# Zero products until the first weights, four banks for the transform, another order of low parts, and the last expert's output by halves

## The reference

```
h = x
layer 0:  h += fourier_mixer(rms_norm(h))        # h @ w_in, 2-D FFT over tokens and 256 channels of a group, real part, @ w_out
          h += (silu(n @ w_gate) * (n @ w_up)) @ w_down          # n = rms_norm(h), 2816 hidden
layer 1:  h += neighbourhood_attention(rms_norm(h))              # 16 heads, 4 x 64 grid, window 16 wide, bias table, @ w_o
          logits = n @ w_router + b_router; top 2 of 8 experts, gates = softmax of the two
          h += sum over the two of gate * (silu(n @ Wg[e]) * (n @ Wu[e])) @ Wd[e]     # 3584 hidden
return rms_norm(h) * final_norm
```

## Time and profile before

| | us |
|---|---|
| three runs | 1366.85, 1367.61, 1368.39 |
| median | 1367.61 |
| the profiled execution | 1367.15 |
| its span | 1365.3 |

### The profile page before, as it was taken

The page is one execution under the profiler, slowest core; times in us unless marked ns, Lnnn a source line. Parts: engine busy times, 40 slices in busy tenths (PEclk is TensorE's granted clock), DMA queues, the critical chain, the costliest instruction groups (busy, mean ns, idle before and its releaser), DMA issues.

```text
span 1365.3 us, 17406 instructions
## 1 busy us (share of the span) xinstructions
PE 1344.7 (98%) x6341; PEld 1117.9 (82%) x6341; DVE 1111.9 (81%) x815; ACT 923.2 (68%) x755; POOL 34.5 (3%) x48
## 2 busy tenths in 40 slices
PE   8999999999999999999999999999999999999997
PEld 7888888787878888888888888888888888888885
DVE  5756666655678889888988988898898889889997
ACT  6554444545647778777777877877787787777774
POOL 0000000000101000000000000000000000002000
PEclk8999999999989999999999999999999999999999
DMA  9666775563339999999999999999999999999992
GB/s 354 246 207 179 210 211 190 175 204 104 101 109 378 383 378 365 395 382 357 398 388 372 373 394 377 358 398 388 368 376 394 367 370 397 381 374 385 396 394 90
DMA packets 194971, 432.32 MB, mean 317 GB/s; under 512 B 19632, under 2 KB 22064, under 8 KB 194800
## 3 DMA queue, kind: packets, MB, share of 16 engines
q1 hardware_dynamic: 178784, 416.28, 83.4%
q0 software_dynamic: 3360, 11.78, 2.2%
q10 hardware_dynamic: 12784, 3.69, 1.8%
HBM read 425.94 MB, written 5.78 MB: 316 GB/s over the span
## 4 chain that ended last, share of the span: by engine, by line
PE 95%; DVE 3%; ACT 1%; issue 1%; DMA 0%; POOL 0%; DVEq 0%; ACTq 0%
PE bank_G L1250 10%; PE bank_G L1252 10%; PE bank_G L1251 10%; PE bank_U L1250 10%; PE bank_U L1252 10%; PE bank_U L1251 10%; PE bank_Y L1250 8%; PE bank_Y L1252 8%; PE bank_Y L1251 8%; PE bank_T L1696 2%; PE bank_T L1250 1%; PE bank_T L1252 1%; PE bank_T L1251 1%; DVE w_lo L753 1%; PE bank_G L1512 0%
## 5 line engine op out<-in xcount | busy, mean ns | idle before, releaser
L753 DVE TENSOR_TENSOR w_lo<-raw,w_hi 128x2048 fp32r<-128x2048 f32 x390 | 885.9, 2289 | 184.6 <-ACT w_hi L458 183.8
L458 ACT ACTIVATE w_hi<-raw 128x2048 fp32r<-128x2048 f32 x390 | 748.6, 1920 | 276.6 <-PE bank_U L1252 98.2
L1250 PE MATMUL bank_Y<-w_hi,hidT_hi 128*128 128x512 f32 x492 | 192.2, 391 | 0.0
L1252 PE MATMUL bank_Y<-w_hi,hidT_lo 128*128 128x512 f32 x492 | 191.6, 389 | 0.0
L1251 PE MATMUL bank_Y<-w_lo,hidT_hi 128*128 128x512 f32 x492 | 191.5, 389 | 0.0
L1250 PE MATMUL bank_U<-w_hi,xg_hi 128*128 128x512 f32 x448 | 179.1, 400 | 0.0
L1250 PE MATMUL bank_G<-w_hi,xg_hi 128*128 128x512 f32 x448 | 175.2, 391 | 1.3 <-DVE xg_lo L774 0.9
L1252 PE MATMUL bank_U<-w_hi,xg_lo 128*128 128x512 f32 x448 | 175.0, 391 | 0.0
L1251 PE MATMUL bank_U<-w_lo,xg_hi 128*128 128x512 f32 x448 | 174.5, 390 | 0.0
L1252 PE MATMUL bank_G<-w_hi,xg_lo 128*128 128x512 f32 x448 | 174.5, 390 | 0.0
L1251 PE MATMUL bank_G<-w_lo,xg_hi 128*128 128x512 f32 x448 | 174.4, 389 | 0.0
(11 more groups left out here) (301 smaller groups left out, 1363.5 us busy)
## 6 DMA issues: line engine op xcount, KB each, us to landing
raw<-in_expert_w_gate SPq DMA_DIRECT2D x112, 1024.0 KB, 7.7
raw<-in_expert_w_up SPq DMA_DIRECT2D x112, 1024.0 KB, 7.8
raw<-in_expert_w_down SPq DMA_DIRECT2D x112, 1024.0 KB, 7.7
raw<-in_nat_w_qkv SPq DMA_DIRECT2D x12, 1024.0 KB, 5.1
raw<-in_ffn_w_gate SPq DMA_DIRECT2D x11, 1024.0 KB, 8.9
raw<-in_ffn_w_up SPq DMA_DIRECT2D x11, 1024.0 KB, 5.7
raw<-in_ffn_w_down SPq DMA_DIRECT2D x11, 1024.0 KB, 5.2
raw<-in_fourier_w_out SPq DMA_DIRECT2D x4, 1024.0 KB, 15.6
```

The source lines that it names most:

```text
L458: nc.scalar.activation(w_hi[w][:], raw[s][:], ACT.Copy).then_inc(hi_made, 1)
L753: nc.vector.tensor_tensor(w_lo[w][:], raw[s][:], w_hi[w][:].bitcast(f32), ALU.subtract).then_inc(lo_made, 1)
L1250: nc.tensor.matmul(out_, xh, wh, start=start, stop=False)
L1252: return nc.tensor.matmul(out_, xl, wh, start=False, stop=stop)
```

## The change

1. `still(23)` in place of `still(12)`.
2. `token_dft` writes four banks in turn (`BY_TOKEN`: T0, T1, G0, G1) and may run four steps ahead of `pt_lo`; `channel_dft` writes `BY_CHANNEL` (Y0, Y1, U0, U1) and waits for no fold.
3. `project` gets `stream`: TensorE waits for `act_lo` by quarter, ahead of the two eighths that use it, for streams 1 and 2. On VectorE, at the end of the dense part, `stream_lo(2, 0)` stands ahead of the split.
4. `gate_weights` is cut in two: `gates` (den, g1, g2) stays in the second step of the last expert; the three operations that make `weight` move to its last step.
5. Last expert: `last_columns(q, rows, first)` makes the left half of the output over all four row blocks, then the right half's first two blocks, `scatter(0)`, the right half's other two, `scatter(1)`. `add_result` goes by halves and counts each addition. The final squares are four of 512 columns; GpSimd adds D x EPS to the left sums and joins the two.

The diff, cut to its core:

```diff
+    BY_TOKEN = [T[0], T[1], G[0], G[1]]
+    BY_CHANNEL = [Y[0], Y[1], U[0], U[1]]
...
+        pool.wait_ge(fin_sq, NB)
+        nc.gpsimd.tensor_scalar(mo["sumsq_half"][:], mo["sumsq_half"][:], D * EPS, None, ALU.add).then_inc(rstd_chain, 1)
+        pool.wait_ge(rstd_chain, 4 + 1 + 1)
         for b in range(NB):
-            pool.wait_ge(sq_done, NB * 4 + b + 1)
-            nc.gpsimd.tensor_scalar(rstd[:, 4, b:b + 1], sumsq[:, 4, b:b + 1], 1.0 / D, EPS, ALU.mult, ALU.add).then_inc(rstd_chain, 1)
+            pool.wait_ge(fin_sq, NB + b + 1)
+            nc.gpsimd.tensor_scalar(rstd[:, 4, b:b + 1], sumsq[:, 4, b:b + 1], mo["sumsq_half"][:, b:b + 1], 1.0 / D, ALU.add, ALU.mult).then_inc(rstd_chain, 1)
...
-                nc.scalar.activation(fo["pt_hi"][:, m % PT], T[m % 2][:], ACT.Copy).then_inc(pt_hi_done, 1)
+                nc.scalar.activation(fo["pt_hi"][:, m % PT], BY_TOKEN[m % 4][:], ACT.Copy).then_inc(pt_hi_done, 1)
...
-        squares(4)
+        for q in range(2):
+            for b in range(NB):
+                act.wait_ge(e_added, NB * q + b + 1)
+                cs = slice(BANK * q, BANK * (q + 1))
+                total = sumsq[:, 4, b:b + 1] if q else mo["sumsq_half"][:, b:b + 1]
+                nc.scalar.activation(mo["hn_hi"][:, b, cs], h[:, b, cs], ACT.Square, accum_out=total).then_inc(fin_sq, 1)
...
             last.then_inc(h_half, 1)
+            if q == 0:
+                stream_lo(2, 0)
             split_past(n - 1 + q)
-            stream_lo(2, q)
+        stream_lo(2, 1)
...
-            for b in range(NB):
-                dve.wait_ge(terms_added, 4 * NB)
-                for q in range(2):
+            for q in range(2):
+                for b in range(NB):
                     dve.wait_ge(e_scatter, NB * (2 * (E - LAST) + q) + b + 1)
+                    dve.wait_ge(terms_added, 4 * NB)
...
                     elif c == 1:
+                        gates()
+                    elif c == STEPS - 1:
                         gate_weights()
...
+                        if stream is not None and b == 0 and kk % 2 == 0:
+                            pe.wait_ge(act_lo_done, 4 * stream + kk // 2 + 1)
...
-                if (n, b) == (0, 0):
-                    pe.wait_ge(act_lo_done, 4 * i + 2)
                 if (n, b) == (0, 1):
                     transpose_stream(i, 1)
-                if (n, b) == (1, 0):
-                    pe.wait_ge(act_lo_done, 4 * i + 4)
...
-        still(12)
+        still(23)
...
-            if m >= 2:
-                pe.wait_ge(pt_lo_done, m - 1)
+            if m >= 4:
+                pe.wait_ge(pt_lo_done, m - 3)
...
-            if g >= 2:
-                pe.wait_ge(ft_channels, 2 * (g - 1))
...
+            def last_columns(q, rows, first=0):
+                c = STEPS - 1
+                if first == 0:
+                    ready(AT["down", c, 0], E)
+                    pe.wait_ge(e_hidT_lo, E * STEPS + (c + 1))
+                for kk in range(first, first + rows):
+                    half, k = kk // KROW, kk % KROW
+                    j = AT["down", c, half]
+                    if q == 0 and half and k == 0:
+                        ready(j, E)
+                    wh, wl = parts(j, E, KROW)
+                    cs = slice(BANK * q, BANK * (q + 1))
+                    last = three(Y[q][:], hidT_hi[c % 2][:, P * kk:P * (kk + 1)], hidT_lo[c % 2][:, P * kk:P * (kk + 1)],
+                                 wh[:, k, cs], wl[:, k, cs], False, kk == BANK // P - 1)
...
-            down(STEPS - 1, 0)
-            down(STEPS - 1, 1)
+            if kept:
+                last_columns(0, 4)
+                last_columns(1, 2)
+                scatter(0)
+                last_columns(1, 2, 2)
...
+            if kept:
+                scatter(1)
```

More of the change, by code:

```diff
@@ L1252, in three, with project @@
             return nc.tensor.matmul(out_, xl, wh, start=False, stop=stop)
-        def project(pieces, banks, width, done, before=lambda n, b: None):
+        def project(pieces, banks, width, done, before=lambda n, b: None, stream=None):
             for n, j in enumerate(pieces):
@@ L1426, in _ @@
             if c == 0:
-                project(at["gate"][0], G, widths[0], d_gate, stream_second(1))
+                project(at["gate"][0], G, widths[0], d_gate, stream_second(1), 1)
             else:
@@ L1720, in down, with scatter @@
                 last.then_inc(piece_used, 1)
+            def last_columns(q, rows, first=0):
[12 more added lines that the diff above has]
+                                 wh[:, k, cs], wl[:, k, cs], False, kk == BANK // P - 1)
+                    if q and k == KROW - 1:
+                        last.then_inc(piece_used, 1)
+                    elif kk == BANK // P - 1:
+                        last.then_inc(e_y, 1)
+            def scatter(q):
+                pe.wait_ge(e_selT_copy, E - LAST + 1)
+                pe.wait_ge(e_ylo, 2 * (E - LAST) + 1 + q)
+                for b in range(NB):
+                    cs = slice(BANK * q, BANK * (q + 1))
+                    bk = T[q] if b == 0 else (G, U)[q][1]
+                    nc.tensor.matmul(bk[:], mo["selT"][:, b], mo["y_hi"][:, cs], start=True, stop=False)
+                    nc.tensor.matmul(bk[:], mo["selT"][:, b], mo["y_lo"][:, cs], start=False, stop=True).then_inc(e_scatter, 1)
             for c in range(STEPS):
@@ L1752, in expert @@
             down(STEPS - 2, 1)
-            down(STEPS - 1, 0)
-            down(STEPS - 1, 1)
+            if kept:
[3 more added lines that the diff above has]
+                last_columns(1, 2, 2)
+            else:
+                down(STEPS - 1, 0)
+                down(STEPS - 1, 1)
             if ahead:
                 first_gate(E + 1)
-            if not kept:
-                return
-            pe.wait_ge(e_selT_copy, E - LAST + 1)
-            for q in range(2):
-                pe.wait_ge(e_ylo, 2 * (E - LAST) + 1 + q)
-                for b in range(NB):
-                    cs = slice(BANK * q, BANK * (q + 1))
-                    bk = T[q] if b == 0 else (G, U)[q][1]
-                    nc.tensor.matmul(bk[:], mo["selT"][:, b], mo["y_hi"][:, cs], start=True, stop=False)
-                    nc.tensor.matmul(bk[:], mo["selT"][:, b], mo["y_lo"][:, cs], start=False, stop=True).then_inc(e_scatter, 1)
+            if kept:
+                scatter(1)
         pe.wait_ge(e_sel, 1)
```

39 lines of the change are left out of this document (20 added, 19 removed).

## The result

The changed kernel takes 1369.66 us (median of 10 runs, 1367.80 to 1372.28), the kernel before 1366.88 us (10 runs, 1365.03 to 1368.39) on the same chip: the ratio is 1.0024, with a 95% interval of 1.0014 to 1.0033. By the medians that is 2.8 us slower; the ratio is not that of the medians (1.0020) and puts it at 3.3. The profiled execution took 1369.06 us with a span of 1367.3, so 2.0 us of span more than the one shown of before.

A forecast was written before the change was run, and what follows sets the result against it. TensorE, busy 98% of the span, was taken as the bound. Terms -2.1 + 1.6 - 0.5 + 2.2 = +1.2 us on the profiled 1367.15 gave 1368.35, taken as 1368.5; range 1365.8 to 1370.8.

The forecast's parts named there:

- within: Whole kernel: time differs from the kernel before by no more than 0.2%, 2.7 us; chance 0.75.
- low parts ahead of a split: Dense end: VectorE idles until the high parts are ready, then splits last, so TensorE starts q/k/v later; +1.6 us.
- Start and transform stage: First projection and transforms: 23 zero products keep the clock full, four banks shorten waits; output projection earlier, -2.1 us.
- The rival of products that come too late: Start: zero products run past the first weights at a low clock; sum +3.6, 1370.8 us; chance 0.15.
- The rival that banks are all that is missing: Transform stage: four banks end both TensorE waits, -4.0 instead of -2.1, 1366.5 us; chance 0.10.
- Finer waits: Dense end and first gate projection: TensorE's waits by quarter gain nothing; 0.
- Gate weights: Last expert: second step loses its wait, -0.5 us; the three operations' new place costs 0 to +0.1.
- Last expert's halves: Last expert's output: waiting for the last split and the scatter between products delay the final scaling; +2.2 us.
- The rival of halves that overlap as drawn: Last expert: the last split comes early enough, so the tail is +0.45, 1366.7 us; chance 0.10.
- All the signs for "right": Trace signs: full clock from 8.65 us, output projection near 44.7, predicted waits near q/k/v and the last split, scaling time.
- slow products after 9 us: Trace sign that the prediction is wrong: products at low clock after 9 us; no size given.
- shifts elsewhere: Remaining case: shifts in other places, such as a clock that falls in another stage; no size, chance 0.05.

The follow-up runs named there:

- e10: The kernel before with only TensorE's waits for the activations' low parts by quarter instead of by half: 1365.46 us, ratio 0.9995.
- e11: The kernel before with waits by quarter and VectorE's new order (low parts ahead of the split) at the dense end: 1370.61 us, ratio 1.0028.
- e4: The changed kernel with VectorE's old order at the dense end and the last expert's old end: 1364.32 us, ratio 0.9983 to the kernel before.
- e7: The changed kernel with the first half's scatter behind all 24 products of the last down projection: 1369.06 us, ratio 1.0020 to the kernel before.
- e6: The kernel before with only four banks for each transform: 1365.36 us, ratio 0.9994.
- e5: The kernel before with only 23 zero products instead of 12: 1366.41 us, ratio 0.9997.
- e2: The changed kernel with 12 identity products on TensorE in its wait ahead of the q/k/v projection: 1368.75 us, ratio 1.0015 to the kernel before.
- e12: The changed kernel once more, unchanged: 1370.00 us (8 runs), ratio 1.0023 to the kernel before.
- e3: The changed kernel with the last expert's old end (products, scatters, adds and squares as before): 1367.84 us, ratio 1.0010 to the kernel before.
- e1: The changed kernel with VectorE's old order (split, then low parts) at the dense end, waits by quarter kept: 1366.45 us, ratio 0.9999 to the kernel before.
- e8: The changed kernel with old dense-end order and old tail, gate weights moved to VectorE's idle time ahead of the last low parts: 1364.08 us, ratio 0.9981.
- e9: As e8, with adds and squares by halves, products and scatters in the old order: 1363.85 us, ratio 0.9978 to the kernel before.

## Why the prediction was right or wrong, point by point

The predicted time, 1368.5 us, is 1.2 below the median of 1369.66, which lies in the range (1365.8 to 1370.8) and, just under its upper end, in the forecast's own (1367.3 to 1369.8). Part of this closeness is luck: the forecast stands on the time of the execution read, 1367.15, and the median of three runs, 1367.61, where ten runs of the kernel before have 1366.88. As a difference the sum said +1.2 us, and +2.8 came, more than double. The 2.8 us are just on the slower side of the bound of 2.7 for which "within" was forecast; "slower" had a chance of 0.17. The sum failed in one term above all, the low parts ahead of a split.

- **Start and transform stage, -2.1.** Measured -1.96. The zero products ended at 8.44 instead of 8.0, the clock stayed full, the output projection began at 44.84 for the predicted 44.7. The path is right: the transforms began at 30.76 instead of 31.2, but VectorE's splits set the rest, and TensorE's two waits are 2.05 us in sum for the predicted 2. The size is right against the one execution that was read, and that is in part luck: its clock was low for the longest time. e10 and e11 have the same start as the kernel before and reached the output projection at 45.57 and 45.27, only 0.7 and 0.4 us behind the changed kernel. By the ratio of e4, 2.3 us in all, less what its trace shows elsewhere (0.8 for the waits by quarter, 0.6 upstream, +0.2 at the end), I estimate about 1 us for the start. The rival of products that come too late did not happen in any of the ten executions with 23 of them; at worst (e7) they held the first real product until 9.19 us, and its clock was full. The rival that banks are all that is missing is half right: they alone reached 44.73 (e6), but 2.1 us were won, not 4.0, since the wait for VectorE stays. The share of each edit can't be given as one number, as I had done: the gains overlap, and zero products alone can turn into a longer wait with a low clock behind it (e5).
- **Low parts ahead of a split, +1.6.** This step failed. The mechanism is as drawn: VectorE idle for 1.62 us (1.5 predicted), the wait 2.99 us (about 3), 1.65 us more (e2, e7). Left out was what TensorE does behind a wait of that length: in four of five executions with it (the changed kernel, e12, e3, e11; not e7) the clock fell to 1.2 GHz, which cost 1.3 to 1.6 us (stages of 9.67 to 9.93 us against 8.34). I had looked at the clock only behind waits of 0.7 us and at the start. The earlier trace rows showed an idle time of 3.08 us and the earlier trace rows a low clock behind it: the hint was there, and I used it for the start alone. The term is +3.1, and alone (e11) it gave a loss of 0.28%.
- **Finer waits, 0.** Right in the new order, where the split ends last. Wrong for the edit itself: with the split first it is worth 0.8 us (e1, e10). At the gate projection it is worth nothing, as predicted: 207.7 us in every trace.
- **Gate weights, -0.5 and 0 to +0.1.** Measured -0.55 upstream and +0.24 at the new place (e8), more than the 0.1 allowed.
- **Last expert's halves, +2.2.** Measured +2.1, in the traces (16.77 less the 14.65 of e3) as in the medians (e1 less e4); the +2.3 of the distance (5) has the gate weights in it. It is made of 1.3 for the scatter in the middle (e7) and about 0.8 for the wait for the last split. The parts were mis-sized against each other: the scatter cost 1.3 and not 1.0 us, and the wait was 0.49 us, 0.66 over the usual pitch, and not 1.0; VectorE did not wait for ScalarE's half of that split, since the gate weights had filled that time. The rival of halves that overlap as drawn falls.

All the signs for "right" came, the wait for the last split at half its size. What spoiled the sum was slow products behind the new wait: the sign "slow products after 9 us" was meant for the start, and a clock that falls in another stage was only named among the 0.05 for shifts elsewhere, without a price. By the Trainium skill (TensorE: Matmul & The Clock Gate, Part 1) the chip's observation of TensorE's activity doesn't begin with the kernel, so where the clock changes varies between executions. The traces agree that it varies: behind the same instructions and the same wait of 2.99 us the clock fell in e12 and not in e7, and with 12 zero products it was low until 14.6 us in one execution and never at the start of another (e11). Why, no run here shows.

## What to carry to other kernels

Where VectorE feeds TensorE with two things, the one whose input is ready goes first, and the other is handed over in pieces; an order that makes VectorE idle for 1.6 us costs that at once. A wait of TensorE has a second price behind it: price any wait that grows to 2 us and more with the slow products that may follow. Filling it with products is worth a try, though e2 alone doesn't prove it. Where the clock differs between executions, as at the start here, one trace of before is no baseline: read a second. An engine that arrives earlier at an unchanged limit only waits longer, so look for the limit first (here the banks and VectorE's splits) and speed up the way to it last.

## What was not expected of the hardware

- The clock fell to 1.2 GHz behind waits of 2.99 us (four of five executions), 3.08 and 2.56 us (the start, before and e6), 2.14 us (e5) and once 1.85 us (the start of e10), and not behind 1.87 and 1.88 us (e11) or 1.37 and less. A fall cost 1.3 to 1.6 us at the dense end and up to 1.8 us in e5 (47.03 against 45.27 in e11).
- The changed kernel's ten runs go with the granted clock: at a mean of 0.990 the span is 1370.3 us (two runs), at 0.995 it is 1366.0 (one run). That isn't all of it: among e12's runs at 0.992 the spans go from 1368.0 to 1370.2 us.
- The low clock of the router stage lasts longer in some executions than in others and moves the stage's length by 1.0 us, once by 1.6 (e9), more than most edits here are worth.
